# Two of the three products of an expert tile made one 512-column product, from tile 48 on

## The reference, cut to what matters

```python
h = jax.nn.gelu(jnp.einsum('thkd,td->thk', u[eidx], xb), approximate=False)
return jnp.einsum('thk,thkd->td', gate * h, v[eidx])
```

## Time and profile before

| | |
|---|---|
| median of three runs | 2639.32 us |
| the profiled execution | 2636.74 us, its span 2634.9 us |
| granted TensorE clock, mean | 0.975 |
| TensorE busy | 2474.0 us (94%) |
| VectorE busy | 1896.4 us (72%) |
| ScalarE busy | 1106.9 us (42%) |
| GpSimd busy | 295.9 us (11%) |

### The profile page before, as it was taken

One profiled execution on the slowest core, in us unless ns is written; L12 is line 12 of the kernel. 1 busy time (PEld: TensorE's weight loads), 2 busy tenths in 40 slices (PEclk: granted clock), 3 DMA queues, 4 the chain that ended last, 5 costly groups with the idle time before them and its releaser, 6 DMA issues.

```text
span 2634.9 us, 41842 instructions
## 1 busy us (share of the span) xinstructions
PE 2474.0 (94%) x16494; PEld 2244.3 (85%) x16494; DVE 1896.4 (72%) x3307; ACT 1106.9 (42%) x1660; POOL 295.9 (11%) x124
## 2 busy tenths in 40 slices
PE   7998999999999999788999999999999688998999
PEld 7877999999988888578999999988888577787987
DVE  6577797788766766768796888766666757546675
ACT  3341344444555555120444444545544263343333
POOL 0000486000000000000695000000000102000000
PEclk9999999999999999889999999999999899899999
DMA  6544677666777777424677666777777441233545
GB/s 218 174 130 138 191 216 206 190 189 190 200 243 257 234 245 241 147 80 141 182 206 202 190 189 190 212 246 252 241 242 243 120 136 41 77 124 121 175 149 173
DMA packets 201427, 483.67 MB, mean 184 GB/s; under 512 B 24080, under 2 KB 93712, under 8 KB 200720
## 3 DMA queue, kind: packets, MB, share of 16 engines
q1 hardware_dynamic: 197632, 472.42, 58.9%
q10 hardware_dynamic: 3600, 8.57, 1.0%
HBM read 446.30 MB, written 34.60 MB: 183 GB/s over the span
## 4 chain that ended last, share of the span: by engine, by line
PE 75%; DVE 11%; POOL 5%; DMA 4%; ACT 3%; issue 2%; ACTq 0%; DVEq 0%; SPq 0%
PE psum L1039 26%; PE psum L992 20%; PE psum L815 19%; POOL rounded L788 5%; PE psum L1015 3%; DVE rounded L1486 3%; DMA sb<-in_u_turned 3%; PE psum L1150 1%; DVE rounded L1482 1%; ACT rounded L2845 1%; ACT rounded L2509 1%; DVE sb L1521 1%; DVE sb L2293 1%; PE psum L973 1%; PE psum L879 1%
## 5 line engine op out<-in xcount | busy, mean ns | idle before, releaser
L1486 DVE TENSOR_TENSOR rounded<-sb,rounded 128x1024 fp32r<-128x1024 f32 (+3 forms) x696 | 816.1, 1175 | 499.4 <-ACT rounded L2845 320.6
L2845 ACT ACTIVATE rounded<-sb 128x1024 fp32r<-128x1024 f32 x512 | 542.8, 1060 | 776.3 <-PE psum L1039 327.6
L992 PE MATMUL psum<-rounded 128*128 128x256 f32 x6144 | 772.2, 285 | 15.0 <-POOL rounded L788 14.8
L992 PEld LDWEIGHTS psum<-rounded 128*128 128x128 f32 x6144 | 744.7, 191 | 18.8 <-POOL rounded L788 18.8
L1039 PE MATMUL psum<-rounded,weights 128*128 128x512 f32 x3072 | 697.5, 389 | 1.7 <-DVE weights L2436 1.3
L1039 PEld LDWEIGHTS psum<-rounded,weights 128*128 128x128 f32 x3072 | 576.4, 188 | 122.1 <-issue 2.8
L815 PE MATMUL psum<-rounded 128*128 128x256 f32 (+1 forms) x3924 | 597.2, 314 | 42.0 <-DVE rounded L1486 33.3
L815 PEld LDWEIGHTS psum<-rounded 128*128 128x128 f32 x3924 | 546.8, 196 | 89.7 <-DVE rounded L1486 27.8
L2509 ACT ACTIVATE rounded<-sb 128x1024 fp32r<-128x1024 f32 (+2 forms) x222 | 206.8, 942 | 323.7 <-PE psum L815 198.4
L788 POOL TENSOR_TENSOR rounded<-sb,rounded 128x1024 fp32r<-128x1024 f32 x96 | 267.3, 2800 | 485.6 <-ACT rounded L2845 485.1
L2427 DVE TENSOR_TENSOR halves<-halves,small 128x768 bf16<-128x768 bf16 x256 | 131.6, 555 | 4.4
(11 more groups left out here) (370 smaller groups left out, 1580.9 us busy)
## 6 DMA issues: line engine op xcount, KB each, us to landing
sb<-in_u_turned SPq DMA_DIRECT2D x256, 512.0 KB, 4.0
sb<-in_peer_v SPq DMA_DIRECT2D x256, 512.0 KB, 3.6
hidden<-sb SPq DMA_DIRECT2D x256, 128.0 KB, 3.9
sb<-hidden SPq DMA_DIRECT2D x256, 128.0 KB, 3.5
sb<-in_ret_w_in SPq DMA_DIRECT2D x48, 512.0 KB, 3.9
sb<-in_ffn_w_up SPq DMA_DIRECT2D x40, 512.0 KB, 4.0
sb<-in_peer_w_q SPq DMA_DIRECT2D x32, 512.0 KB, 3.8
sb<-in_ffn_w_down SPq DMA_DIRECT2D x22, 512.0 KB, 3.7
```

Of the source, the lines that this page charges most:

```text
L992: mm = pe.matmul(ps(bank, 1)[:, 0:T], u[p][:, k * P:(k + 1) * P], hT[:, q, k, :], start=(k == 0 and w == 0), stop=(k == KD - 1 and w == 2))
L1486: vec.tensor_tensor(ring_lo[0:k, part, 0:wide], ring[0:k, slot, 0:wide], ring_hi[0:k, part, 0:wide].bitcast(F32), ALU.subtract).then_inc(c ...
L2845: act.activation(ring_hi[:, n % SPLIT, :], ring[:, n % RING, :], ACT.Copy).then_inc(tile_hi, 1)
```

## The change

From tile 48 on (`WIDE_FROM`) the hi weights are multiplied with both parts of the tokens in one product of 512 columns, which fills the bank: the hi x hi sums in columns 0 to 255, the hi x lo sums in 256 to 511. The lo weights times the hi tokens stay a product of 256 columns that adds to the first half. A tile then has 16 products in place of 24. The two halves have to be added up: ScalarE copies the upper half to `small_sum` (`small_half`), VectorE adds it to the lower half and writes `hid` (`add_halves`), and ScalarE takes the gelu of `hid` in place one turn later (`wide_hidden(i - 1)`). `small_sum` is 256 columns of a scratch area, in which four other small tiles move to make room.

```diff
+WIDE_FROM = 48
@@ TensorE, hidden(i)
+                    if i >= WIDE_FROM:
+                        for k in range(KD):
+                            pe.matmul(ps(bank, 1).rearrange("p (q t) -> p q t", q=2), u[0][:, k * P:(k + 1) * P], hT[:, :, k, :],
+                                      start=(k == 0), stop=False, skip_group_check=True)
+                            mm = pe.matmul(ps(bank, 1)[:, 0:T], u[1][:, k * P:(k + 1) * P], hT[:, 0, k, :], start=False,
+                                           stop=(k == KD - 1), skip_group_check=True)
+                        mm.then_inc(chunks_done, 1)
+                        return
@@ VectorE
+                def add_halves(i):
+                    vec.wait_ge(small_out, wide_before + i - WIDE_FROM + 1)
+                    vec.tensor_tensor(hid[:, i % 3, :], small_sum, ps(HIDDEN_BANKS[i % 4], 1)[:, 0:T], ALU.add).then_inc(*own.mark(summed))
@@ VectorE, after lower_tile(first_u + i + 3)
+                    if WIDE_FROM <= i < NK:
+                        add_halves(i)
@@ ScalarE
+                def small_half(i):
+                    if wide_before + i > WIDE_FROM:
+                        act.wait_ge(summed, wide_before + i - WIDE_FROM)
+                    if i >= 3:
+                        act.wait_ge(hid_stored[i % 3], stored_by(d0, i - 3))
+                    act.wait_ge(chunks_done, first_u + i + 1)
+                    act.activation(small_sum, ps(HIDDEN_BANKS[i % 4], 1)[:, T:2 * T], ACT.Copy).then_inc(small_out, 1)
+
+                def wide_hidden(i):
+                    act.wait_ge(summed, wide_before + i - WIDE_FROM + 1)
+                    act.activation(hid[:, i % 3, :], hid[:, i % 3, :], ACT.Gelu).then_inc(gelu_done, 1)
@@ ScalarE, after round_tile(first_u + i + 3)
-                    if i < NK:
+                    if i < WIDE_FROM:
                         hidden(i)
+                    elif i < NK:
+                        small_half(i)
+                        if i > WIDE_FROM:
+                            wide_hidden(i - 1)
+                        if i == NK - 1:
+                            wide_hidden(i)
...
```

More of the change, by code:

```diff
@@ L337, in build @@
         misc = lasting.take(512)
-        norm_cols = misc[:, 128:128 + KD * (2 * 4 + 4)]
+        norm_cols = misc[:, 132:132 + KD * (2 * 4 + 4)]
+        small_sum = misc[:, 228:228 + T]
         rounded = nc.alloc_sbuf_tensor_at("rounded", [P, 2 * KD * T + 2 * SPLIT * SLOT], F32R,
@@ L359, in build @@
         iota_half = small_parts.take(P)
-        doubled = nc.alloc_sbuf_tensor_at("doubled", [P, 2 * P], BF16, offset=SB_AT + 4 * (misc_at + 276))
+        doubled = nc.alloc_sbuf_tensor_at("doubled", [P, 2 * P], BF16, offset=SB_AT + 4 * (misc_at + 4))
         iota_two = Memory(doubled, 0, 2 * P).take(P, 2)
@@ L392, in build @@
         gates_placed = sem("gates_placed")
+        summed, small_out = sem("summed"), sem("small_out")
         gelu_done, multiplied = sem("gelu_done"), sem("multiplied")
@@ L1840, in rooted @@
                 done()
-            top8, sum8 = misc[:, 256:264], misc[:, 264:272]
+            top8, sum8 = misc[:, 488:496], misc[:, 496:504]
             def vec_mla(a, phase):
@@ L2428, in onehots @@
                                           ALU.mult).then_inc(*(own.mark(onehots_made) if q else own.next()))
+                def add_halves(i):
+                    vec.wait_ge(small_out, wide_before + i - WIDE_FROM + 1)
+                    vec.tensor_tensor(hid[:, i % 3, :], small_sum, ps(HIDDEN_BANKS[i % 4], 1)[:, 0:T], ALU.add).then_inc(*own.mark(summed))
+                wide_before = (NK - WIDE_FROM) * peers_before[phase]
                 def apply_gates(i):
@@ L2766, in act_mixers @@
                 hi_to(end["mix_out"] + 2)
-            sum8_ = misc[:, 264:272]
+            sum8_ = misc[:, 496:504]
             def act_cross(a):
```

## The result

The changed kernel takes 2644.0 us (median of 17 runs, 2640.33 to 2649.41) against 2639.26 us of the kernel before on the same chips (17 runs, 2635.51 to 2643.97): ratio 1.0019, 95% interval 1.0011 to 1.0026. It is 5 us slower; 2628.7 us was forecast, in a range of 2622 to 2637. The profiled execution has a span of 2638.4 us, 3.5 more than before.

What follows compares the result with a forecast made beforehand. TensorE's stream was taken to bound the kernel, VectorE next. Products -17.1 us and seam +6.5 us gave -10.6 us, so 2639.3 became 2628.7 us, with an 8-in-10 range of 2622 to 2637.

Steps and rivals of the forecast that it cites:

- the product term: TensorE's `_u` tiles from 48 on: 16 products save 0.107 us a tile, 17.1 us over 160 tiles; bounds 0 and 34.
- The seam: Passage from the last `_u` tiles to `_v` tile 0: two delays stop being hidden, 6.5 us for both layers, bounds 3.8 to 12.1.
- the forecast's own range: Total time of 2623 to 2634 us, from the seam's 3.8 to 12.1 and some 2 us between medians; chance 0.71.
- part (a): `_v` tile 0 waits for tile 127's gelu, now behind the addition; TensorE resumes at 3.6 us, loss 1.9 us a layer.
- part (b): SyncE's queue: stores of late gelus hold back the first `_v` loads, adding 1.35 us a layer.
- VectorE's addition: Adding the halves takes 0.46 us a tile (0.34 at the low end); VectorE stays under TensorE, 96% full, cost 0.
- Rival 3: Tiles 48 to 122: additions make VectorE the bound and the kernel slower, 2651 us at 0.75 us each; chance 0.07.
- Rival 1: TensorE's idle time at the seam drops the clock to 1.2 GHz, 3 to 6.4 us in all, 2632 to 2635; chance 0.12.
- Rival 2: The wide-narrow pair gains little or nothing: 2645.8 us if it costs three narrow products, 2637 at half gain; chance 0.10.
- Rival 4: The change doesn't do what it says; the order has 16 products a tile from 48 on, so no chance of its own.

Runs made afterwards that it cites:

- experiment 1: Changed kernel with wide and narrow products kept, but gelu of columns 0 to 255 straight away, upper half never read; ratio 0.9979 to the kernel before.
- experiment 7: Changed kernel with the first six `_v` loads ahead of the stores of tiles 122 to 127 in SyncE's queue; ratio 0.9998 to the kernel before.
- experiment 2: As experiment 1, but the wide product reads 512 token columns side by side instead of two runs; ratio 0.9979 to the kernel before.
- experiment 3: As experiment 1, but each tile's eight wide products come first, its eight narrow ones behind; ratio 0.9954 to the kernel before.
- 10: As experiment 1, but two wide products and then their two narrow ones in turn; ratio 0.9951 to the kernel before.
- experiment 4: Changed kernel with 24 products of 256 columns a tile again, hi x lo in the upper half, halves added up; ratio 1.0045 to the kernel before.
- experiment 6: Changed kernel with the wide form only in the last eight tiles of each layer; ratio 1.0038 to the kernel before.
- 9: As 8, but wide form in tiles 48 to 125 and six first `_v` loads ahead of the stores; ratio 0.9961 to the kernel before.
- 11: As 9, but two wide and two narrow products in turn; ratio 0.9956 to the kernel before.
- 8: Changed kernel with wide products first, halves added, wide form in tiles 48 to 119 only; 2627.99 us, ratio 0.9952 to the kernel before.

## Why the prediction was wrong

**The step that failed is the size of the product term:** "I take 17.1, since both widths have that excess each time." Measured are 6.2 us, by the start of the second half (2 x 3.1), and the same 6.2 with nothing but the pairs changed (experiment 1). Two things take the other 11:

- A pair is 353 ns and not 226.7 + 120.0 = 346.7. The wide product behind a narrow one takes about 236, the narrow one behind a wide one about 117. That is 0.05 us a tile, 8 us over 160 tiles. I had the excess of either width from streams of that width alone. Half of the change could be read in the trace of the kernel before: at its seam the first five wide products behind narrow ones take 234, 235, 229, 232 and 231 ns. The earlier trace rows show them only merged, six products in 1.55 us.
- In the 64 tiles a layer that have a group of gates in front, the old form was cheaper than 24 x 120 behind its first product: read one by one, the seven that follow the first take 116 to 121 ns, 13 ns less in sum. Taking products away there saved less: before to after 3.63 to 3.59, where 3.63 to 3.52 was forecast; a tile without gates went from 2.88 to 2.82, against 2.77. A tile with gates thus misses its forecast by 0.07 us and one without by 0.05; the 0.02 between them, of which those 13 ns are the larger part, makes the other 2 to 3 us over 128 tiles.

The bounds I gave this term, 0 and 34 us, hold the 6.2. But the forecast's own range, 2623 to 2634, carried the seam's bounds and the medians' 2 us alone (added up, 2624 to 2636); a term whose operation no row showed had its middle taken as certain. With 6.2 in its place and all else as written, the forecast is 2639.3 - 6.2 + 6.5 = 2639.6, no change.

**Where the Trainium skill stood.** Its 2.5 ns a product (TensorE: Matmul & The Clock Gate, "Wait — 56ns, not 53.3ns?") gave an estimate of 3.2 us for the term, nearer to the 6.2 than mine. It is not confirmed by that: the excess of a stream is 13.3 ns in this trace, and the two-and-two order has 6.6 us a layer, 13.2 in both, out of the same number of products.

**The seam was right in kind and nearly in size:** +6.5 us was forecast and +7.3 found. For part (a), TensorE was to resume at 3.6 us, and experiment 7 shows 3.50. For part (b), these are SyncE's queue and ScalarE's roundings of the first layer in the changed kernel:

```profile
714.68 0.32 SPq L678 DMA_DIRECT2D sb<-hidden  x1
715.05 0.42 SPq L658 DMA_DIRECT2D sb<-in_peer_v  x1
...
719.75 1.06 ACT L2864 ACTIVATE rounded<-sb 128x1024 fp32r<-128x1024 f32 x1 [3.01 <-DMA sb<-in_peer_v]
725.99 1.06 ACT L2864 ACTIVATE rounded<-sb 128x1024 fp32r<-128x1024 f32 x1 [1.26 <-DMA sb<-in_peer_v]
728.67 0.42 ACT L2888 ACTIVATE sb<-sb 128x256 f32<-128x256 f32 x1 [1.05 <-DVE sb L2443]
```

TensorE ends tile 122 at 708.43 (the start of the gates behind it). The load of `_v` tile 0 goes out 6.6 us later (6.2 forecast), its rounding starts at 11.3 (10.0), that of tile 2 at 17.6 (16.2), and the gelu of tile 127 comes behind it and the addition. In the second layer TensorE resumes at 4.86 us, where 3.6 + 1.35 = 4.95 was forecast; in the first at 5.91, by the later landings, inside the bounds.

**VectorE's addition cost nothing, as forecast.** Starts in the changed kernel:

```profile
600.32 0.41 DVE L2443 TENSOR_TENSOR sb<-sb,psum 128x256 f32<-128x256 f32 x1
600.65 0.42 DVE L2432 TENSOR_TENSOR halves<-doubled,small 128x512 bf16<-128x512 bf16 x1
```

It is 0.33 us to the next start, the low bound and not the 0.46 that I took: reading PSUM did not make it longer than its neighbour in the earlier trace rows that reads none. TensorE waits 1.4 us for the first one-hots, as before, and for none behind them, and with tiles of 3.59 us VectorE is at 90%, not 95. Rival 3 (0.07) fell.

**Rival 1, the clock at the seam (0.12), came true in part:** once in two layers, 1.5 us, behind 4.34 us of idle time; 3 to 6.4 us had been forecast for both. Its "7 to 15 such products" came from no row; a fall here costs what 7 such products lose. **Rival 2 (0.10) is what happened in size:** the pair gave a third of its gain, somewhat under its "half the gain 2637". Of its two reasons, the two runs of tokens fall with experiment 2. The alternation is borne out in kind: experiments 3 and 10 order the same 16 products otherwise and gain 3.0 us or more a layer on the pairs where the clock stays up. What in TensorE makes it so is open. The Trainium skill's sentence on non-contiguous patterns (PSUM — Partial Sum Buffer, "Specifications") stands among the properties of PSUM, and the two runs are of an operand in SBUF; so experiment 2 neither bears it out nor speaks against it. **Rival 4** had nothing to it: there are 1280 products fewer.

**The balance** is -6.2 + 7.3 + 1.5 = +2.6 us by the traces, against 5.0 timed. The kernels with a longer wait at the seam come out above their traced sums each time, by 1 to 3 us (experiments 4, 6 and 7, and this one); all but this one, which lies 0.3 us outside, are inside their intervals. But without such a wait experiments 9 and 11 are 1.5 and 1.2 us above theirs too, and 3 and 8 are 1.5 and 1.8 below. Whether that wait has a further cost elsewhere stays open.

## What to carry to other kernels

The cost of an instruction between neighbours of another shape is not in a stream of its own shape: when a change interleaves two shapes, put the alternation's cost in the range at its bounds, or order the work so that equal shapes stand side by side (here two and two was enough). And look at the ends of a loop that is made deeper by one stage: the same edit lost at the seam, in 8 of 80 tiles, all that it gained in the other 72, and leaving those 8 as they were turned a loss of 5 us into a gain of 6, and with the wide products first into one of 12.7 (9.2 to 16.4).

## What the hardware showed that I had not expected

- **A ramp in product spacing.** With a weight load for each fp32r product, a wide one directly behind a narrow one takes 232 to 241 ns, and only from the sixth wide one in a row on is it 226 or 227; a narrow one directly behind a wide one takes 113 to 120 in the pairs, 113 to 117 behind two or more wide ones, and in a row they go up to 120. Neither the operand in two runs, nor the count of changes alone, nor the bank explains it. The cause is open.
- **The clock and short idle times.** It fell to its 1.2 GHz level behind idle times of TensorE of 4.46, 4.34 and 4.24 us, but also behind 2.48 (experiment 6) and 2.28 (experiment 3, second layer). It did not behind 3.54 (experiment 4, first layer), 3.29 (changed kernel, second layer) and 1.93. So the length of the gap alone does not decide it in these runs. Each fall cost 1.5 to 1.6 us.
